# A two-layer block: the input projection at 512 columns, in two halves of K around the scores

## The reference

```
xn   = rms_norm(x) * norm_g
proj = xn @ w_in                 # 1024 x 4096: q, k, v, z for two attentions
D heads (4): softmax(q1 k1 + bias) - lam * softmax(q2 k2 + bias), times v, rms norm, * silu(z)
N heads (8, in 4 pairs): attention over a window of a 16 x 64 grid, * silu(z)
x    = x + concat(D, N) @ w_out
```

## Time and the profile before

| what | us |
|---|---|
| median of 3 runs | 3199.08 (3197.17 to 3201.27) |
| span of the profiled execution | 3193.0 |
| TensorE busy in it | 3109.5 |
| VectorE, ScalarE, GpSimd busy | 2028.7, 1058.5, 1420.3 |
| attention of layer A, first to last sigmoid | 92.4 to 668.6 |

### The profile page before, as it was taken

One profiled execution on the slowest core, in us unless ns is written; L12 is line 12 of the kernel. 1 busy time (PEld: TensorE's weight loads), 2 busy tenths in 40 slices (PEclk: granted clock), 3 DMA queues, 4 the chain that ended last, 5 costly groups with the idle time before them and its releaser, 6 DMA issues.

```text
span 3193.0 us, 51486 instructions
## 1 busy us (share of the span) xinstructions
PE 3109.5 (97%) x19108; PEld 2705.6 (85%) x19108; DVE 2028.7 (64%) x3766; ACT 1058.5 (33%) x2057; POOL 1420.3 (44%) x1207
## 2 busy tenths in 40 slices
PE   9999999999989999999999999999999999999998
PEld 8898989988987889888888888988889888888886
DVE  4757576665788212687777775455553777777766
ACT  3545454541124210422222221544341422222221
POOL 5434344316643334665555545411104755555534
PEclk9999999999999999999999999999999999999999
DMA  7211201143112112111111111000002011111111
GB/s 199 75 56 38 67 28 54 38 172 97 67 34 63 52 45 68 38 59 47 53 53 53 53 53 63 7 21 17 18 21 93 27 53 53 53 53 53 53 52 53
DMA packets 181828, 179.58 MB, mean 56 GB/s; under 512 B 50234, under 2 KB 163066, under 8 KB 181498
## 3 DMA queue, kind: packets, MB, share of 16 engines
q1 hardware_dynamic: 181566, 177.02, 17.4%
q10 hardware_dynamic: 96, 0.26, 0.0%
HBM read 160.12 MB, written 22.38 MB: 57 GB/s over the span
## 4 chain that ended last, share of the span: by engine, by line
PE 63%; DVE 2%; issue 1%; ACT 1%; POOL 0%; POOLq 0%; DVEq 0%; ACTq 0%
PE banks L2692 16%; PE banks L79 13%; PE banks L81 13%; PE banks L80 13%; PE banks L3509 2%; PE banks L3486 1%; PE banks L215 1%; PE banks L3443 0%; PE banks L3444 0%; PE banks L3425 0%; POOL x L183 0%; PE banks L3452 0%; PE banks L2314 0%; DVE x L2929 0%; POOL rstd L178 0%
## 5 line engine op out<-in xcount | busy, mean ns | idle before, releaser
L2929 DVE TENSOR_TENSOR x<-x,banks 128x512 f32<-128x512 f32 x784 | 523.2, 687 | 242.2 <-PE banks L2692 233.7
L79 PE MATMUL banks<-winbuf_hi,xt_hi 128*128 128x256 f32 x1024 | 302.2, 295 | 11.7 <-ACT qkn L933 5.5
L80 PE MATMUL banks<-winbuf_lo,xt_hi 128*128 128x256 f32 x1024 | 290.0, 283 | 0.0
L81 PE MATMUL banks<-winbuf_hi,xt_lo 128*128 128x256 f32 x1024 | 290.0, 283 | 0.0
L79 PEld LDWEIGHTS banks<-winbuf_hi,xt_hi 128*128 128x128 f32 x1024 | 196.1, 191 | 33.5 <-issue 13.0
L79 PE MATMUL banks<-h1t_hi,f1w_buf_hi 128*128 128x512 f32 x512 | 199.5, 390 | 1.6 <-issue 1.6
L79 PE MATMUL banks<-h3t_hi,f2w_buf_hi 128*128 128x512 f32 x512 | 199.5, 390 | 1.6 <-issue 1.6
L81 PE MATMUL banks<-h3t_hi,f2w_buf_lo 128*128 128x512 f32 x512 | 199.2, 389 | 0.0
L81 PE MATMUL banks<-h1t_hi,f1w_buf_lo 128*128 128x512 f32 x512 | 199.2, 389 | 0.0
L80 PE MATMUL banks<-h1t_lo,f1w_buf_hi 128*128 128x512 f32 x512 | 199.2, 389 | 0.0
L80 PE MATMUL banks<-h3t_lo,f2w_buf_hi 128*128 128x512 f32 x512 | 199.2, 389 | 0.0
(11 more groups left out here) (545 smaller groups left out, 9339.6 us busy)
## 6 DMA issues: line engine op xcount, KB each, us to landing
f1w_raw<-in_w_ff SPq DMA_DIRECT2D x32, 1024.0 KB, 5.1
f2w_raw<-in_w_ff SPq DMA_DIRECT2D x32, 1024.0 KB, 5.1
winraw<-in_w_in SPq DMA_DIRECT2D x128, 128.0 KB, 3.3
gluw_raw<-in_ssm_w_glu SPq DMA_DIRECT2D x14, 512.0 KB, 4.6
x<-in_x SPq DMA_DIRECT2D x8, 512.0 KB, 6.3
wow_raw<-in_w_out SPq DMA_DIRECT2D x4, 1024.0 KB, 5.9
x<-in_x SPq DMA_DIRECT2D x1, 4096.0 KB, 15.2
gew_raw<-in_w_ple_gate SPq DMA_DIRECT2D x4, 1024.0 KB, 4.8
```

What stands on the lines that cost most here:

```text
L79: nc.tensor.matmul(out, a.hi, b.hi, start=start, stop=False)
L80: nc.tensor.matmul(out, a.hi, b.lo, start=False, stop=False)
L81: return nc.tensor.matmul(out, a.lo, b.hi, start=False, stop=stop)
L2929: nc.vector.tensor_tensor(xx, xx, chip.ps[:, 4 + 2 * (p % 2) + g, :], ALU.add).then_inc(s_acc, 1)
```

## The change

- Three buffers serve the weight chunks instead of two pairs and one landing buffer. Each chunk lands in what becomes its low part, and GpSimd splits it in place. A chunk's load waits for the last round of the chunk three before it.
- A round of two chunks makes 512 columns: the moving operand takes 256 columns from each of two buffers, and the whole of bank 6 is written. The list `ROUNDS` says which: chunk 0 alone in 8 rounds, chunk 1 alone for 4 tiles, chunks 1 and 2 for 4 tiles, then in unit u for tiles 0 to 3 the chunks 2u + 2 and 2u + 3, for tiles 4 to 7 the chunks 2u + 3 and 2u + 4 (in unit 6 chunk 15 alone). That is 56 rounds of two chunks and 16 of one. The heads of a unit are so made from tile 4 on, half a unit earlier than the values.
- Each step has one round, cut into two halves of K: k 0 to 3 behind `transposes`, k 4 to 7 behind `scores`. In step 7 the scores of the next unit's step 0 stand between the halves. Nothing stands ahead of `transposes`.
- ScalarE copies the round out behind both exps of its step (two or three copies: heads need a square and a copy). The squares come behind that.
- VectorE and GpSimd have one head tile a step (`a` = 8(u + 1) + t + 3) instead of two in each of the first four steps. GpSimd splits chunks 2u + 4 and 2u + 5 during unit u.
- The heads of odd units' tiles 4 to 7 get a place of their own (`qkn_odd`).

```diff
+    ROUNDS = [((0,), j) for j in range(NT)] + [((1,), j) for j in range(4)] + [((1, 2), j) for j in range(4, NT)]
+    for u in range(NU - 1):
+        for t in range(NT):
+            pair = (2 * u + 2, 2 * u + 3) if t < 4 else (2 * u + 3, 2 * u + 4)
+            ROUNDS.append((tuple(c for c in pair if c < 2 * NU), t))
+    TAKEN = [sum(len(cs) for cs, _ in ROUNDS[:r]) for r in range(len(ROUNDS) + 1)]
+    PROLOGUE = 2 * NT
+
+    def last_round(c):
+
+        return max(r for r, (cs, _) in enumerate(ROUNDS) if c in cs)
...
+    def pair_rows(cs, k):
+
+        a, b = sorted(c % 3 for c in cs)
+        hi = m.win_hi[:, 16 * a + k:16 * b + k + 1:16 * (b - a), :]
+        first, last = (Mixers.LOWS[n] - Mixers.LOWS[0] + k for n in (a, b))
+        return Pair(hi, m.win_lo[:, first:last + 1:last - first, :])
...
+            def weights(c):
+                if c >= 2 * NU:
+                    return
+                if c >= 3:
+                    sp.wait_ge(s_p, last_round(c - 3) + 1)
+                for piece in range(4):
+                    for h, col in enumerate(columns(c)):
+                        sp.dma_start(m.raw[c % 3][:, 2 * piece:2 * piece + 2, h * P:h * P + P],
+                                     w_in[:, 2 * piece:2 * piece + 2, col:col + P]).then_inc(s_win[c % 3][piece], 16)
...
             for u in range(NU):
                 for t in range(NT):
-                    g = NT * u + t
+                    g, a = NT * u + t, NT * (u + 1) + t + 3
                     if g and kind_of(g - 1) == "D":
                         root(g - 1)
-                    if u < NU - 1 and t < 4:
-                        head_roots(NT * (u + 1) + 2 * t)
+                    if a < NT * NU:
+                        head_roots(a)
                     if t < 2:
                         gate(u, t)
-                    if u < NU - 1:
-                        if 4 * (2 * u + 3) + t < 8 * NU:
-                            split(4 * (2 * u + 3) + t)
-                        if t < 4:
-                            head_roots(NT * (u + 1) + 2 * t + 1)
+                    if 4 * (2 * u + 4) + t < 8 * NU:
+                        split(4 * (2 * u + 4) + t)
...
+            def project(r, ks=range(KT)):
+                cs, j = ROUNDS[r]
+                if r == 0 or cs != ROUNDS[r - 1][0]:
+                    pe.wait_ge(s_split, 4 * (max(cs) + 1))
+                if cs == (0,):
                     pe.wait_ge(s_xl, 2 * (j + 1))
-                pe.wait_ge(s_pe, n)
...
+                pe.wait_ge(s_pe, TAKEN[r])
+                if len(cs) == 2:
+                    out, rows = chip.ps[:, 6, :].rearrange("p (a n) -> p a n", a=2), pair_rows
+                else:
+                    out, rows = chip.ps[:, 6, 0:CH], lambda cs, k: chunk_rows(cs[0], k)
+                for k in ks:
+                    last = mm3(nc, out, m.xt.at(slice(None), k, slice(j * P, j * P + P)), rows(cs, k), k == 0, k == KT - 1)
+                if ks[-1] == KT - 1:
+                    last.then_inc(s_p, 1)
...
                     more = u < NU - 1
-                    if more:
-                        project(n)
-                        if t == 7:
-                            scores(g + 1)
-                    elif t < 7:
+                    if not more and t < 7:
                         keep_going(t, 3)
-                    else:
+                    elif not more:
                         begin_output(0)
                     transposes(g)
+                    if more:
+                        project(PROLOGUE + g, range(KT // 2))
                     if t < 6:
                         scores(g + 2)
                     if more:
-                        project(n + 1)
+                        if t == 7:
+                            scores(g + 1)
+                        project(PROLOGUE + g, range(KT // 2, KT))
...
+            def taken(r):
+                cs, j = ROUNDS[r]
+                act.wait_ge(s_p, r + 1)
+                for c in sorted(cs):
+                    src = banked(cs, c) if len(cs) == 2 else chip.ps[:, 6, 0:CH]
+                    (values_taken if c % 2 else heads_taken)(c // 2, j, src)
...
                     more = u < NU - 1
-                    if more:
-                        taken(n)
                     evacuate(g)
...
                     if t < 7:
-                        if more:
-                            taken(n + 1)
                         if t == 1 and u and UNITS[u - 1][0] == "D":
                             out_hi(u - 1, 1)
                         if t == 4 and UNITS[u][0] == "D":
                             out_hi(u, 0)
                         if t < 6:
                             expo(g + 2, 0)
+                            down(g + 2)
+                            expo(g + 2, 1)
+                        if more:
+                            taken(PROLOGUE + g)
                         squares(g)
                         if more and t in (5, 6):
                             head_hi(u + 1, 2 * (t - 5))
                             head_hi(u + 1, 2 * (t - 5) + 1)
-                        if t < 6:
-                            down(g + 2)
-                            expo(g + 2, 1)
...
-                    if more and t < 4:
+                    if a < NT * NU:
                         head_sums(a)
-                    if more and 1 <= t <= 4:
-                        head_scale(a - 1)
```

More of the change, by code:

```diff
@@ L350, in __init__ @@
         self.yt = chip.pair("yt", 0, [P, KT, SEQ])
-        self.w = [chip.pair(f"winbuf{b}", 64 + 16 * b, [P, KT, CH]) for b in range(2)]
-        self.raw = at("winraw", 96, [P, KT, CH])
+        self.win_hi = at("winhi", 64, [P, 40, CH], F32R)
+        self.win_lo = at("winlo", self.LOWS[0], [P, 110, CH], F32R)
+        self.w = [Pair(self.win_hi[:, 16 * b:16 * b + KT, :],
+                       self.win_lo[:, self.LOWS[b] - self.LOWS[0]:self.LOWS[b] - self.LOWS[0] + KT, :]) for b in range(3)]
+        self.raw = [at(f"winraw{b}", self.LOWS[b], [P, KT, CH]) for b in range(3)]
         self.s = at("scores", 104, [P, 2, 2, SEQ])
@@ L416, in stage_mixers, with head_tile, head_taken, head_rows @@
     w_in = io["w_in"].rearrange("(k p) n -> p k n", p=P)
+    ROUNDS = [((0,), j) for j in range(NT)] + [((1,), j) for j in range(4)] + [((1, 2), j) for j in range(4, NT)]
[7 more added lines that the diff above has]
+        return max(r for r, (cs, _) in enumerate(ROUNDS) if c in cs)
+    def head_tile(a):
+        u, i = a // NT, a % NT
+        return u, (i if u == 0 else (i + 4) % NT)
+    def head_taken(a):
+        u, j = head_tile(a)
+        r, = (r for r, (cs, tile) in enumerate(ROUNDS) if 2 * u in cs and tile == j)
+        return TAKEN[r] + 1 + sorted(ROUNDS[r][0]).index(2 * u)
+    def head_rows(u, j):
+        return m.qkn_odd[:, j - 4, :] if j >= 4 and u % 2 else m.qkn[:, j, :]
+    def chunk_rows(c, k):
+        return m.w[c % 3].at(slice(None), k, slice(None))
+    def pair_rows(cs, k):
[3 more added lines that the diff above has]
+        return Pair(hi, m.win_lo[:, first:last + 1:last - first, :])
+    def banked(cs, c):
+        part = sorted(x % 3 for x in cs).index(c % 3)
+        return chip.ps[:, 6, part * CH:(part + 1) * CH]
     def kind_of(g):
@@ L447, in stage_mixers @@
         s_xin = sems(nc, ctx, "mxx", " ".join(str(j) for j in range(NT)))
-        s_win = sems(nc, ctx, "mxw", "0 1 2 3")
+        s_win = [sems(nc, ctx, f"mxw{b}", "0 1 2 3") for b in range(3)]
         s_sst = sems(nc, ctx, "mxst", "0 1 2 3")
@@ L512, in _ @@
             sp.dma_start(m.xgain[:, :], row_bcast(io["norm_g"])).then_inc(s_xg, 16)
-            for piece in range(4):
-                weights(piece)
+            weights(0)
             for j in range(1, NT):
@@ L527, in _ @@
             sp.dma_start(io["s_rpb"], m.wide[:, :]).then_inc(s_wide, 16)
-            for piece in range(4, 8):
-                weights(piece)
+            weights(1)
             sp.wait_ge(s_bv, 4)
@@ L533, in _ @@
             spread_strip(sp, 0)
-            for piece in range(8, 12):
-                weights(piece)
+            weights(2)
             strips(0)
+            weights(3)
             sp.wait_ge(s_wide, 16)
@@ L542, in _ @@
             for u in range(NU - 1):
-                for t in range(4):
-                    weights(4 * (2 * u + 3) + t)
+                weights(2 * u + 4)
                 if u:
@@ L548, in _ @@
                     edges(0)
+                weights(2 * u + 5)
                 if u < NU - 2:
-                    for t in range(4):
-                        weights(4 * (2 * u + 4) + t)
                     sp.wait_ge(s_add, 2 * (NT * u + NT))
                     (strips if UNITS[u][0] == "D" else edges)(UNITS[u][1] + 1)
-            sp.wait_ge(s_p, 2 * NT * NU)
+            sp.wait_ge(s_p, len(ROUNDS))
             sp.wait_ge(s_split, 8 * NU)
@@ L932, in taken @@
                     act.wait_ge(s_qt, 4 * u)
-                nc.scalar.activation(m.qkn[:, j, :], src, ACT.Copy).then_inc(s_pe, 1)
```

(12 more changed lines are left out.)

77 lines of the change are left out of this document (33 added, 44 removed).

## The result

The changed kernel takes 3306.24 us (median of 4 runs, 3298.91 to 3308.3) where the kernel before takes 3198.12 on the same chip (4 runs, 3196.95 to 3201.27): a ratio of 1.0336, 95% interval 1.0321 to 1.035. It is slower by 108 us; forecast were 45, with 3265 us as the upper end. The profiled execution has a span of 3304.6 us, 111.6 more than before.

A forecast was written before the change was run, and what follows sets the result against it. TensorE's row of work was taken to set each unit. Terms -17 + 28 + 6 + 5 + 25 = +47 us, less 2 for the last D unit, gave +45 on 3199: 3244 us, range 3210 to 3265.

The forecast's parts named there:

- the counts that were to show them: Profile after: 256-column projection matmuls fall from 3072 to 384, beside 1344 of 512 columns; D units not under 88 us.
- the likeliest case: The forecast itself, whole kernel: 3244 us, 45 us slower on the span; chance 0.50.
- Term 1: Projection rounds: 56 pair rounds of 512-column matmuls replace 112 rounds, saving 0.30 us each, 17 us in all.
- Term 2: Ends of steps 5 and 6, seven units: `transposes` directly behind the q and k turns wait 2.0 us for `qklo`, +28 us.
- term 5: D units: the loop through bank 6 gets as long as the step, ScalarE's queued work delays steps; +6.5 a unit, +25 us.
- Terms 3 and 4: N units' step 1, 2.5 us wait for `ystage_lo` against 0.5, +6; step 7 before a D unit, later scores, +5.
- term 4: Step 7 before a D unit: the next unit's first scores come later, 1.7 us lost, three times, +5 us.
- rival D: Whole kernel heavier: bank 6 loop at its bound (+15), late splits (+10), or falling clock (+14); 3265 to 3285 us, chance 0.10.
- Costed at nothing: Four pair rounds moved into the prologue (10.3 us there, as much less in unit 6), unit 0's first `transposes`, loads, head roots.
- A: Rival, only the forced waits: terms 1 to 4 with term 5 hidden, +22, 3221 us; chance 0.27.
- B: Rival, a gain: TensorE stays the bound and today's waits go, -33, 3166 us, or 3182 with term 1 alone; chance 0.08.

The follow-up runs named there:

- e5: Kernel before (256 columns, two rounds a step) with only its first round moved behind `transposes` and ScalarE's copy of it behind bank 4's copy: 3291.89 us, ratio 1.0296.
- e6: Changed kernel with the first half round back ahead of `transposes` and ScalarE's old order back (copies ahead of exps, squares between them): 3185.48 us, ratio 0.9962.
- e8: e6 with every 512-column matmul of the pair rounds made as two of 256 columns: 3193.87 us, ratio 0.9992.
- e3: Changed kernel with ScalarE's whole old order back (copies ahead of exps, squares and `qkhi` before the second exp), TensorE's order staying changed: 3269.02 us, ratio 1.022.
- e7: e6 with the next unit's first scores put ahead of `transposes` in step 7: 3181.81 us, ratio 0.9951.
- e1: Changed kernel with short idle matmuls into bank 0 where TensorE waited longest, fewer than the waits hold: 3286.88 us, ratio 1.0282.
- e9: Changed kernel with the `transposes` blocks that write bank 7 put after six others in five-block N steps; block order also changed in D units: 3293.07 us, ratio 1.0306.
- e10: e3 with idle filler matmuls as in e1, none ahead of the late halves: 3246.06 us, ratio 1.0155.

## Why the prediction was right in its sign and too small

The direction and the main reason hold, and so do the counts that were to show them (576 instances of each of the three lines are 1344 of 512 columns and 384 of 256; D units are far over 88 us): the projection round had been the cover of results made just before, and behind `transposes` it no longer covers them. e5 shows it by itself, and e6, with both orders put back, loses nothing. What was wrong is the size; 63 of 108 us were missing. Three steps failed: the list of what `transposes` wait for left out bank 7, terms 1 and 5 were mis-sized, and the clock was left out of the likeliest case.

Forecast and measurement by place, the forecast worked out from the terms. (By these a D unit comes to 87.2 - 2.4 + 4.0 + 6.5 = 95.3 us and an N unit to 78.5 - 2.4 + 4.0 + 2.0 + 1.7 = 83.8; the 93 or 94 and 82 or 83 that stand in the forecast were 1 to 2 us under its own terms.)

| place | terms | measured | missing |
|---|---|---|---|
| first `transposes` of unit 0, 85.55 to 98.24 | +10 | +12.7 | 2 |
| D units of pairs 0 to 2 (102.0, 103.2, 103.3) | +24 | +46.7 | 22 |
| N units of pairs 0 to 2 (91.2, 91.2, 91.3) | +16 | +38.0 | 22 |
| last D unit, 82.1 to 95.2 | -5 | +13.1 | 18 |

**Term 1, the width, was mis-sized.** It measured 8.4 us (e8), not 17. The row chosen, 15 steps inside one long group, has no edges; the change cuts the work into groups of 12, and each pays them again. The forecast saw "2.8 with its edge" and still summed by the pitch. 8 to 9 us of what was missing.

**Term 2, q and k.** Right. 14 waits of 2.0 were forecast. The profile after has 14 with 31.8 us in total, e5 and e3 14 with 27.8 and 28.1. The longer ones, up to 3.6 us, stand ahead of D units' step 6, where `qkhi` is late; the forecast had that in term 5.

**Terms 3 and 4.** The wait behind `ystage_lo` in N units' step 1 was forecast with 2.5 us and measured 2.81, under the name of `yheads`: VectorE's copy of the values is queued behind `ystage_lo`, and `transposes` of the next step needs both. Ahead of D units' step 5 it is 2.4, four times (2.5 forecast). Of term 4 the profile after has the wait for `combine` ahead of step 0 (0.8 us where 0.9 stood); the whole was not measured by itself; in e6 the late scores cost 3.7 us in seven such steps, if e7's whole gain is theirs.

**The step that failed for N units: the list of waiters.** The forecast followed bank 4's and bank 5's waits and overlooked `s_out`. In an N step with five key blocks the fifth of either head is turned into bank 7, where `values` of the step before was written, and VectorE must have copied that out. Ahead of step 5 (TensorE, then VectorE):

```profile
444.02 1.31 PE L843 MATMUL banks<-probsT,vz 128*64 128x128 f32 x20
447.33 0.41 PE L821 MATMUL banks<-ident,scores 128*128 128x128 f32 x2 [2.00 <-DVE yheads L1232]
```

```profile
445.96 1.03 DVE L1246 TENSOR_TENSOR ystage_lo<-yheads,ystage_hi 128x512 fp32r<-128x512 f32 x1 [0.80 <-ACT ystage_hi L1040]
446.89 0.29 DVE L1232 COPY yheads<-banks 128x128 f32<-128x128 f32 x1
```

The copy is made at 446.89, behind `ystage_lo`, and TensorE has stood still for 2.00 us. The kernel before shows this wait too, 1.2 us in all; a round of 2.97 us used to lie in it. Ahead of steps 3 and 4 the wait is 0.49, so with the 2.00 some 3.0 us a unit, and 0.3 more than forecast ahead of step 2: 10 us in three units. At full clock (e1) an N unit takes 88.0 us, 4.2 above the 83.8 of the terms; this wait and the 1.2 us of width that were not gained make about as much. e9 covers 0.65 us of each such wait and gains 11 to 13, some of it clock.

**The term that was mis-sized for D units: term 5.** Mechanism right: without ScalarE's new order (e3) the unit is 89.7 us long and TensorE no longer waits for bank 6. Size at full clock: of e1's 99.2 us, 87.2 are the kernel before, less 1.2 for the width, plus 4.0 for term 2; 9.2 are left where 6.5 stood (e1 less e3 gives 9.5). That is 11 to 12 us over the four units, and the bound of the forecast, +40 for all four, held it. Step by step, from one `transposes` to the next:

```
              0      1      2      3      4      5      6      7     sum
D  before  10.98  10.63  10.39  10.75  11.91  12.19  10.76   9.57   87.2
D  e1       9.97  13.46  11.37  12.55  13.52  16.77  11.18  10.38   99.2
```

Steps 5 to 7 grew by 5.8 us, and the terms give 5.8 for them (-0.9 for the width, +4.0 for term 2, +0.9 and +1.8 of term 5). Steps 0 to 4 grew by 6.2, and the terms give 2.4 (-1.5, +2.5 for the loop, +1.4 ahead of step 5). Of the 3.8 between them 0.8 is the width; the other 3 are the part that failed, the walk through the loop in the early steps. One link that its list does not name can be seen, in e1 (ScalarE's first exp of three successive steps, then VectorE):

```profile
305.65 1.15 ACT L1012 ACTIVATE scores<-scores,mixsmall 128x1024 f32<-128x1024 f32 x1 [6.96 <-DVE mixsmall L1182]
318.22 1.15 ACT L1012 ACTIVATE scores<-scores,mixsmall 128x1024 f32<-128x1024 f32 x1 [6.51 <-DVE mixsmall L1182]
328.67 1.15 ACT L1012 ACTIVATE scores<-scores,mixsmall 128x1024 f32<-128x1024 f32 x1 [5.33 <-DVE mixsmall L1182]
```

```profile
311.32 1.10 DVE L1254 TENSOR_TENSOR ystage_lo<-yheads,ystage_hi 128x512 fp32r<-128x512 f32 x1 [0.80 <-ACT ystage_hi L1048]
314.65 2.21 DVE L1210 SCALAR_TENSOR_TENSOR scores<-scores,mixsmall 128x1024 f32<-128x1024 f32 x1
325.35 1.53 DVE L1210 SCALAR_TENSOR_TENSOR scores<-scores,mixsmall 128x1024 f32<-128x1024 f32 x1
```

The loop takes 12.57 us and then 10.45, where 9.8 or 10.7 were forecast. In the second, the sum starts 7.13 us after the exp, as the forecast has it (8.5 less 1.4 for the bias); in the first 9.00, since VectorE there also waits 0.80 us for `ystage_hi` of the N unit before and makes its `ystage_lo` for 1.10. The remaining 1 us of a D unit was not traced to a link.

**The clock.** It stood in rival D with 2 us a unit and +14 in all, taken there as rare: 20 is what e1 and e10 give (19.4 and 23.0). The forecast gave this rival 0.10, although it had itself forecast some twenty waits of 2 us and more. This is the second thing that the likeliest case lacked: a cost that follows from its own terms.

**Costed at nothing.** No wait for the loads appeared, right. The four rounds moved into the prologue were put at nothing, 10.3 us there against as much less in unit 6. The first `transposes` comes 12.7 us later; TensorE waits 2.56 us for `combine` ahead of it, where the kernel before did not wait. And this was not given back: the last D unit, which by the pitches should lose 16 x 2.88 - 4 x 5.46 - 4 x 2.88 = 12.7, is 95.2 long, and even in e6 it is 75.3 against 82.1, a gain of 6.8. In steps 4 to 7 a half is only 1.44 us long there (12 x 0.120) and covers less: of the 12 us that TensorE waits over e6's whole loop, 6.2 lie in this unit, most of them for `qklo`, `ystage_lo` and `yheads`. Some 6 us or more.

Together: 45 forecast, 8 for the width, 10 for bank 7, 12 for term 5, 20 for the clock, 6 for the last D unit, 2 for the start make 103 of the 108 to 111. These prices come from different kernels and share some time (e9's gain has clock in it), so they are a budget and no exact sum; the rest, and where in the last D unit it lies, is open.

**The rivals.** A (3221) falls, as term 5 is real. B, the gain, was right on one point: TensorE can stay the bound. e6 and e7 have the same widths, buffers and head work, with D units of 82 us and N units of 77 to 78, at 3185 and 3182. What the forecast of B asked for, the added waits gone, takes an order in which half a round stands ahead of `transposes` and the copy ahead of the exps; even so the gain is 0.4 to 0.5%. D comes nearest in kind, though it priced 3265 to 3285.

## What to carry to other kernels

Work that stands between a producer and its waiter on an in-order engine is cover, and moving it costs every wait that it hid: list all semaphores that the uncovered instruction waits on, those of its output buffers too, and walk each. Where a buffer is freed by an engine that does other things, the order on that engine is the other half of the same edit; test both together, since either alone may show little (1 us and 37, but 121 as a pair). And a price per instruction read from the middle of a long group lacks the two edges that shorter groups pay.

## What the runs showed of the hardware

- The granted clock fell with waits of under 3 us. In the kernel after, TensorE's longest wait between 98 and 750 us is 2.8 us, and the mean clock there is 0.94; in e6, whose waits over the loop add up to some 12 us, it is 1.00. Ahead of the stretch at 0.51 stand the waits of 2.00 and 1.99 us that ended at 447.33 and 461.07. Filling such waits with small matmuls gave 19.4 us back in e1 (clock 0.99 over the loop) and 23.0 in e10 (1.00).
- A group of matmuls has edges. At 512 columns (e6) the first to the second start are 0.32 to 0.35 us, the others 0.23, and from the last to the next group 0.23 to 0.32. At 256 columns (e8) these are 0.20 to 0.22 and 0.12, and 0.12:

```profile
305.01 0.38 PE L79 MATMUL banks<-winhi,xt_hi 128*128 128x256 f32 x1
305.23 0.28 PE L80 MATMUL banks<-winlo,xt_hi 128*128 128x256 f32 x1
305.35 0.28 PE L81 MATMUL banks<-winhi,xt_lo 128*128 128x256 f32 x1
```

- The Trainium skill ("TensorE: Matmul & The Clock Gate", Back-to-back issue gap) gives about 131 ns for each matmul of 512 columns in a sustained stream with weight loads. No stream here shows it: 0.227 us in the output product of the kernel before and 0.226 to 0.232 in the halves of e6 at full clock, nearer to the 216 ns that the same section gives for an isolated one.
